# GpSimd makes a row's product in four pieces, one piece between two gathers that it issues

## The chip, the cores and the metric

The kernel runs on one core of one Trainium2 chip. The metric is the device time of one execution in microseconds (us), lower is better. The kernel before takes 3039.48 us, the median of three runs (3039.14 to 3041.27).

## The reference, cut to what matters

Two transformer blocks on 256 tokens of width 2048. The last step of the second block is a lookup among 16,384 experts, each with one row in the table `u` and one in the table `v` (2048 float32 values, 8 KB a row). For each token 8 heads pick 16 experts each, so 128 per token. A token's result is the sum over its experts of a weight times the `v` row, and the weight is the softmax gate times gelu of the dot product of the token's vector with the `u` row:

```python
def block(args):
    xb, eb, gb = args                     # 128 tokens
    a = jnp.einsum('nd,nhkd->nhk', xb, jnp.take(u_tab, eb, axis=0))
    w = (gb * jax.nn.gelu(a)).astype(xb.dtype)
    return jnp.einsum('nhk,nhkd->nd', w, jnp.take(v_tab, eb, axis=0))
```

The picks come from two rounds of top-16 per head over products of queries and keys.

## The kernel before, in words

The first 1750 us are dense products, whose weights stream in 1 MB chunks. The change lies in the lookup behind them.

**Tiles.** The 256 tokens are two blocks of 128, and a token is a partition. One "row" `q` of the kernel is a tile of 128 partitions by 2048 float32 (1 MB): slot `s` of all 128 tokens of a block, gathered by one indirect DMA that GpSimd issues (line 621). There are 512 rows in this order: 128 of `u` for block 0 (`q` 0 to 127), 128 of `v` for block 0, then the same for block 1.

**Buffers.** There are 14 row buffers (`GATH`). Row `q` goes into the buffer of row `q - 14`, so GpSimd waits before the gather of `q` until row `q - 14` is used (`row_free`). The gathers are issued in order, by one engine.

**Who uses a row.** A `u` row is multiplied with the token's vector and summed over its 2048 columns. VectorE does that in one instruction (`dot`, line 2677). Of the first 118 rows, those with `q % 6 == 3` (3, 9, ..., 117: 20 rows) are made by two other engines: GpSimd multiplies in place (line 606, `multiply`), and ScalarE adds up the product (line 1750), which sets the row free (`row_summed`). A `v` row is scaled and added by VectorE (line 2726), every fourth by TensorE through a diagonal matrix (line 1190).

**Order on GpSimd.** After the gather of row `q`, GpSimd makes the product of row `q - 8` if that is one of its rows. Before it, it waits until that row has landed. What stands behind it, the gather of `q + 1` first, waits until the product is done.

**What else VectorE does here.** Between its dot products it makes the picks of the heads in groups (`choose`), one step after every fourth slot: for the rest of block 0 while the `u` rows of block 0 come in, for block 1 while the `v` rows of block 0 do. The steps are the top-16 searches (lines 2612 to 2618), a cast of the positions (2628), candidate sums (2631), and the pick of the indices by comparison (2641 to 2653). The first three rows are dotted against the vector in SBUF, the others against a copy of it in PSUM (`xn_ps`).

Of the kernel before, what the change touches and what calls it, by code (L numbers as in the profile page):

```python
# [7 lines left out]
ALU = mybir.AluOpType  # L8
# [13 lines left out]
CW = 512  # L22
# [49 lines left out]
ROW_CHUNK = (0, 0, 1, 1, 2, 2, 3, 3, 4, 4, 4, 4, 4, 4)  # L72
FIRST_ROWS = 3
SHARE = 4
POOL_SHARE, POOL_UNTIL, POOL_BEHIND = 6, 118, 8
GELU_AT, GATES_AT = 96, 60
LAST_ROWS = 12
GROUPS = 4
# [27 lines left out]
def used_by(plan, m):  # L106

    return max(p for p, (k, _) in enumerate(plan) if k == m) + 1
# [13 lines left out]
def ada_slot(c):  # L122

    return (c + 1) % ADA_SLOTS
# [79 lines left out]
def by_pool(q):  # L204

    return q < POOL_UNTIL and q % POOL_SHARE == POOL_SHARE // 2
# [11 lines left out]
def lin(const, i=None, step=0):  # L218

    return const if i is None else i * step + const  # L220


def build(nc, a, out):
    with ExitStack() as ctx:
        sems = {}

        def sem(name):
            if name not in sems:
                sems[name] = ctx.enter_context(nc.semaphore(name))
            return sems[name]  # L230
# [28 lines left out]
        def view(name, where, off, shape, dt=F32):  # L259
            return nc.alloc_sbuf_tensor_at(name, [P] + shape, dt, offset=arena_at + 4 * (region[where] + off))  # L260
# [113 lines left out]
        XN2 = view("XN2", "P", 0, [NB, D])  # L374
# [43 lines left out]
        def row(q):  # L418
            return rows_g[:, ROW_AT[q % GATH], :]

        def row_landed(q):

            return sem(f"row_landed{q % GATH}"), 16 * (q // GATH + 1)

        def row_free(q):

            if by_tensor(q):
                return split_used, NCH + consumed(q)
            if by_pool(q):
                return sem("row_summed"), consumed(q)  # L430
            return sem("row_used"), consumed(q)
# [109 lines left out]
        @block.gpsimd  # L541
        def _(pool):
            pool.wait_ge(x_landed[X_PARTS - 1], 16)
            pool.dma_start(wa[:, :, :], a["wa"]).then_inc(sem("mixer_landed"), 16)
            pool.dma_start(wx[:, :, :], a["wx"]).then_inc(sem("mixer_landed"), 16)
            pool.dma_start(decay[:, :, :], a["decay"]).then_inc(sem("mixer_landed"), 16)
            pool.dma_start(rope[:, :, :, :], a["rope"]).then_inc(sem("mixer_landed"), 16)

            pool.wait_ge(sem("ret_s_ready"), 4)
            for dst, name in ((pool_t, "pool_t"), (sgu_w, "sgu_w"), (pool_w, "pool_w"), (keys, "keys"), (mask, "mask"),  # L550
                              (wg, "wg")):
                pool.dma_start(dst[tuple(slice(None) for _ in dst.shape)], a[name]).then_inc(sem("tables_landed"), 16)
            pool.wait_ge(sem("y1_ready"), 2 * LB)
            pool.dma_start(c_row[:, :, :].rearrange("p r k -> p (r k)"), a["c_rows"].partition_broadcast(P)).then_inc(
                sem("c_row_landed"), 16)

            def load_ada(c, s):
                pool.dma_start(ada_w[s][:, :], a["ada"][c]).then_inc(ada_landed[s], 16)  # L558

            for c in range(ADA_SLOTS):  # L560
                load_ada(c, ada_slot(c))
            pool.dma_start(fnw[:, :], a["fnw"].partition_broadcast(P)).then_inc(sem("tables_landed"), 16)
            for c in range(ADA_SLOTS, C_STEP):
                before = c - ADA_SLOTS
                if before < C_FIRST:
                    pool.wait_ge(sem("ada_dots"), used_by(ADA_OUT, before))
                else:
                    pool.wait_ge(sem("ada_dots"), D_FIRST + used_by(ADA_FIRST, before - C_FIRST))
                load_ada(c, ada_slot(c))
            with pool.Fori(0, ADA_LOOPS) as i:  # L570
                for m in range(9):
                    if m < ADA_SLOTS:
                        used = used_by(ADA_STEP, 9 + m - ADA_SLOTS)
                    else:
                        used = D_STEP + used_by(ADA_STEP, m - ADA_SLOTS)
                    pool.wait_ge(sem("ada_dots"), lin(used, i, len(ADA_STEP)))
                    load_ada(lin(C_STEP + m, i, 9), ada_slot(C_STEP + m))
            for m in range(len(ADA_END)):
                if m < ADA_SLOTS:
                    used = D_END - len(ADA_STEP) + used_by(ADA_STEP, 9 + m - ADA_SLOTS)  # L580
                else:
                    used = D_END + m - ADA_SLOTS + 1
                pool.wait_ge(sem("ada_dots"), used)
                load_ada(C_END + m, ada_slot(C_END + m))

            pool.wait_ge(sem("ada_dots"), ADA_DOTS)
            pool.dma_start(ctx_x[:, :, :], a["ctx"].rearrange("o (b p) d -> p (o b) d", p=P)).then_inc(
                sem("ctx_landed"), 16)
            pool.wait_ge(sem("mod_kept"), 1)
            for r in range(4):  # L590
                pool.dma_start(mod_rows[r, :].rearrange("(k p) -> k p", p=P), mod_t[0:KT, r, :]).then_inc(sem("rows_stored"), 16)
            pool.wait_ge(sem("cols_ps"), 2)
            pool.dma_start(sgu_n[:, :], a["sgu_n"].partition_broadcast(P)).then_inc(sem("ctx_landed"), 16)
            pool.wait_ge(sem("rows_stored"), 16 * 4)
            pool.wait_ge(sem("h_ready"), NB * 2 * MH)
            for r, made in enumerate((gb1, gb2)):
                pool.dma_start(made[:, :], mod_rows[r, :].partition_broadcast(P)).then_inc(sem("rows_loaded"), 16)
            pool.wait_ge(sem("rows_loaded"), 16 * 2)
            pool.wait_ge(sem("y2_ready"), KT)
            for r, made in enumerate((sc_row, sh_row)):  # L600
                pool.dma_start(made[:, :], mod_rows[2 + r, :].partition_broadcast(P)).then_inc(sem("rows_loaded"), 16)

            def multiply(q):
                pool.wait_ge(*row_landed(q))
                pool.wait_ge(sem("xn2_ready"), 1)
                pool.tensor_tensor(row(q), row(q), XN2[:, 0, :], ALU.mult).then_inc(sem("pool_made"), 1)  # L606

            for p, (table, b) in enumerate((("u_tab", 0), ("v_tab", 0), ("u_tab", 1), ("v_tab", 1))):
                for s in range(SLOTS):
                    q = p * SLOTS + s  # L610
                    if table == "u_tab" and s % GSTEP == 0:
                        pool.wait_ge(sem("idx_ready"), b * GROUPS + s // GSTEP + 1)
                        pool.sem_inc(sem("gathers"), 1)
                    if q < GATH:
                        if not ROW_CHUNK[q]:
                            pool.wait_ge(sem("xn2_ready"), NB)
                        pool.wait_ge(split_used, NCH - SLOTS_W + ROW_CHUNK[q])
                    else:
                        pool.wait_ge(*row_free(q - GATH))
                    pool.sem_inc(sem("gathers"), 1)  # L620
                    pool.indirect_dma_start(  # L621
                        out=row(q), out_offset=None, in_=a[table],
                        in_offset=bass.IndirectOffsetOnAxis(ap=idx[:, b, s:s + 1], axis=0),
                    ).then_inc(row_landed(q)[0], 16)
                    if q >= POOL_BEHIND and by_pool(q - POOL_BEHIND):
                        multiply(q - POOL_BEHIND)
            pool.wait_ge(sem("sum_kept"), 1)
            pool.tensor_tensor(gated_v[:, 1, :], gated_v[:, 1, :], gb2[:, :], ALU.mult).then_inc(sem("pool_made"), 1)
            pool.wait_ge(sem("pool_made"), POOL_MADE + 1)
            pool.tensor_tensor(X[:, NB - 1, :], X[:, NB - 1, :], gated_v[:, 1, :], ALU.add).then_inc(sem("pool_made"), 1)  # L630
# [1176 lines left out]
        def _(dve):  # L1807
# [492 lines left out]
            def updates(S, steps, banks=ALLB):  # L2300

                u0, depth = upd[0], len(banks) // MKT
                todo = [(d, n, h) for _, d, n in steps for h in range(MH)]

                def weigh(q):
# [583 lines left out]
```

## Time and profile before

| | us |
|---|---|
| median of the runs | 3039.48 |
| profiled execution | 3039.09 |
| its span, first to last instruction | 3037.3 |
| GpSimd busy in the span | 654.1 |
| VectorE busy in the span | 2463.1 |
| product on GpSimd, 128 x 2048, 20 of them, mean | 4.524 |
| issue of a gather of `u` on GpSimd, 256 of them, mean | 0.976 |
| dot product on VectorE, 128 x 2048, mean | 2.285 |
| sum on ScalarE, 128 x 2048, 20 of them, median | 1.912 |

The page gives a busy share for each engine and for 40 equal slices of the span. GpSimd's issue of a gather counts as busy there; the transfer itself is in the lines DMA and GB/s. The whole-span shares average stages with different limits, so the views that count are those of the stretch in which the 20 products are made, 1740 us to 2040 us.

### The profile page before, as it was taken

Reading aid. Unit: us, or ns where it says so; the run is one execution under the profiler, and the core shown is the slowest. Engines: PE = TensorE matmul, PEld = TensorE weight load, DVE = VectorE, ACT = ScalarE, POOL = GpSimd, SP = SyncE. Lnnn points to the kernel's source line nnn. Section 1 sums busy time; section 2 is a strip of 40 time slices with the busy share of each in tenths; the row PEclk is TensorE's granted clock in tenths of the full one; section 3 lists DMA queues with packets and bytes.
Section 4 is the critical chain, followed back from the end, with each engine's and each line's share of the span. In section 5 each row is a group of like instructions: output and inputs, shape, how many; then the busy total and the mean of one; then the engine's idle time right before and its main releaser. Section 6 shows DMA issues by size and latency. Waiting matters only on the chain.

```text
span 3037.3 us, 24749 instructions
## 1 busy us (share of the span) xinstructions
PE 2115.9 (70%) x8578; PEld 1586.2 (52%) x8578; DVE 2463.1 (81%) x2630; ACT 888.1 (29%) x931; POOL 654.1 (22%) x656
## 2 busy tenths in 40 slices
PE   9999999999999999999999910004656200015653
PEld 7888888888888887888788800001212000002221
DVE  6675688999999887575566899979997899987677
ACT  5544443333334366534455311110000000000001
POOL 0000000000000000000000176773333343333332
PEclk9999999999999999999999955556676655557676
DMA  6454778888988965344354699999999999999997
GB/s 247 173 199 168 296 270 321 330 339 333 337 329 328 343 242 174 145 153 156 125 208 166 223 415 396 418 422 421 421 422 422 422 422 422 422 422 422 421 421 307
DMA packets 133192, 958.53 MB, mean 316 GB/s; under 512 B 14833, under 2 KB 15153, under 8 KB 17137
## 3 DMA queue, kind: packets, MB, share of 16 engines
q0 software_dynamic: 89824, 650.98, 52.7%
q1 hardware_dynamic: 43136, 305.91, 27.4%
q8 instruction: 49, 0.80, 0.1%
q10 hardware_dynamic: 146, 0.53, 0.0%
q14 instruction: 37, 0.30, 0.0%
HBM read 955.23 MB, written 2.13 MB: 315 GB/s over the span
## 4 chain that ended last, share of the span: by engine, by line
PE 57%; DMA 25%; DVE 13%; issue 3%; POOL 2%; ACT 1%; SPq 0%; POOLq 0%; DVEq 0%; ACTq 0%
DMA rows_g<-in_v_tab_dram,idx 18%; PE bank L647 17%; PE bank L651 17%; PE bank L648 17%; DVE rows_g L2677 8%; DMA rows_g<-in_u_tab_dram,idx 6%; PE bank L1190 2%; POOL rows_g L621 2%; PE bank L681 1%; DVE bank L2726 1%; PE bank L1004 0%; DMA raw<-in_wstream_dram 0%; PE bank L950 0%; PE bank L689 0%; PE bank L860 0%
## 5 line engine op out<-in xcount | busy, mean ns | idle before, releaser
L1815 DVE TENSOR_TENSOR WL<-raw,WH 128x2048 fp32r<-128x2048 f32 x287 | 657.1, 2291 | 290.7 <-ACT WH L1204 284.8
L1190 PE MATMUL bank<-rows_g,diag 128*128 128x512 f32 x488 | 363.9, 915 | 725.2 <-DMA rows_g<-in_v_tab_dram,idx 725.2
L647 PE MATMUL bank<-WH,UH 128*128 128x512 f32 x1952 | 770.4, 395 | 3.3 <-DVE WL L1815 2.9
L651 PE MATMUL bank<-WH,UL 128*128 128x512 f32 x1952 | 761.1, 390 | 0.0
L648 PE MATMUL bank<-WL,UH 128*128 128x512 f32 x1952 | 760.3, 389 | 0.0
L1204 ACT ACTIVATE WH<-raw 128x2048 fp32r<-128x2048 f32 x287 | 550.3, 1918 | 679.3 <-DMA raw<-in_wstream_dram 665.8
L1190 PEld LDWEIGHTS bank<-rows_g,diag 128*128 128x128 f32 x488 | 139.2, 299 | 950.7 <-issue 660.3
L2677 DVE CUSTOM_DVE_ANT_0 rows_g<-rows_g,bank 128x2048 f32<-128x2048 f32 x233 | 524.8, 2285 | 36.6 <-DMA rows_g<-in_u_tab_dram,idx 36.0
L2726 DVE SCALAR_TENSOR_TENSOR bank<-rows_g,gate_w,bank 128x2048 f32<-128x2048 f32 x193 | 454.5, 2355 | 116.5 <-DMA rows_g<-in_v_tab_dram,idx 98.1
L647 PEld LDWEIGHTS bank<-WH,UH 128*128 128x128 f32 x1952 | 367.0, 188 | 79.6 <-issue 2.6
L651 PEld LDWEIGHTS bank<-WH,UL 128*128 128x128 f32 x1952 | 366.7, 188 | 76.9
L648 PEld LDWEIGHTS bank<-WL,UH 128*128 128x128 f32 x1952 | 367.1, 188 | 74.6
L621 POOL DMA_INDIRECT rows_g<-in_u_tab_dram,idx x256 | 249.8, 976 | 432.7 <-DVE dots L2677 201.7
L621 POOL DMA_INDIRECT rows_g<-in_v_tab_dram,idx x256 | 241.7, 944 | 389.0 <-PE bank L1190 217.2
L2090 DVE CUSTOM_DVE_ANT_0 ada_out<-ada_w,c_row 128x2048 f32<-128x2048 f32 x128 | 292.6, 2286 | 0.0
L558 POOL DMA_DIRECT2D ada_w<-in_ada_dram x96 | 50.9, 530 | 697.7 <-DVE ada_sum L2090 697.7
L1767 ACT ACTIVATE diag<-ident,gate_w 128x128 f32<-128x128 f32 x61 | 24.4, 402 | 555.1 <-PE bank L1190 554.6
L647 PE MATMUL bank<-WH,FH 128*128 128x512 f32 x320 | 124.7, 390 | 1.5 <-DVE X L2158 1.5
L651 PE MATMUL bank<-WH,FL 128*128 128x512 f32 x320 | 124.5, 389 | 0.0
L648 PE MATMUL bank<-WL,FH 128*128 128x512 f32 x320 | 124.5, 389 | 0.0
L1750 ACT ACTIVATE rows_g<-rows_g 128x2048 f32<-128x2048 f32 x20 | 38.2, 1911 | 235.4 <-POOL rows_g L606 235.4
L1178 PE MATMUL bank<-nfin,ident 1*128 1x512 f32 x8 | 7.2, 1076 | 142.5 <-DMA nfin<-in_nfin_dram 142.5
(409 smaller groups left out, 1618.2 us busy)
## 6 DMA issues: line engine op xcount, KB each, us to landing
raw<-in_wstream_dram SPq DMA_DIRECT2D x288, 1024.0 KB, 4.9
ada_w<-in_ada_dram POOLq DMA_DIRECT2D x96, 1024.0 KB, 7.5
rows_g<-in_u_tab_dram,idx POOLq DMA_INDIRECT x256, 24.0
rows_g<-in_v_tab_dram,idx POOLq DMA_INDIRECT x256, 30.1
X<-in_x_dram SPq DMA_DIRECT2D x4, 512.0 KB, 9.9
c_row<-in_c_rows_dram POOLq DMA_DIRECT2D x1, 2048.0 KB, 8.6
ctx_x<-in_ctx_dram POOLq DMA_DIRECT2D x1, 2048.0 KB, 10.4
gb<-mod_rows POOLq DMA_DIRECT2D x2, 1024.0 KB, 5.6
```

The source lines that it names most:

```text
L558: pool.dma_start(ada_w[s][:, :], a["ada"][c]).then_inc(ada_landed[s], 16)
L621: pool.indirect_dma_start(out=row(q), out_offset=None, in_=a[table], in_offset=bass.IndirectOffsetOnAxis(ap=idx[:, b, s:s + 1], axis=0),). ...
L647: pe.matmul(o, ah[:, k0 + k, t], wh[:, w], start=first and k == 0, stop=False)
L648: mm = pe.matmul(o, ah[:, k0 + k, t], wl[:, w], start=False, stop=al is None and last and k == nk - 1)
L651: mm = pe.matmul(o, al[:, k0 + k, t], wh[:, w], start=False, stop=last and k == nk - 1)
L1190: mm = pe.matmul(bank[c], diag[:, n % 2, :], row(q)[:, c * CW:(c + 1) * CW], start=s == mine[0], stop=s == mine[-1])
L1204: act.activation(WH[:, n % SLOTS_W, :], raw[:, n % SLOTS_W, :], ACT.Copy).then_inc(hi_ready, 1)
L1750: act.activation(row(q), row(q), ACT.Copy, accum_out=dots[:, 0, q:q + 1]).then_inc(sem("row_summed"), 1)
L1815: dve.tensor_tensor(WL[:, n % SLOTS_W, :], raw[:, n % SLOTS_W, :], WH[:, n % SLOTS_W, :].bitcast(F32), ALU.subtract).then_inc(lo_ready, 1)
L2090: dve.tensor_tensor_reduce(ada_out[:, :], ada_w[ada_slot(c)][:, :], c_row[:, r, :], 1.0, 0.0, ALU.mult, ALU.add, ada_sum[:, p:p + 1]).then ...
L2677: dve.tensor_tensor_reduce(row(q), row(q), x, 1.0, 0.0, ALU.mult, ALU.add, dots[:, b, q % SLOTS:q % SLOTS + 1]).then_inc(sem("row_used"), 1)
L2726: ins = dve.scalar_tensor_tensor(v_ps, row(q), w, v_ps, ALU.mult, ALU.add)
```

## The change

GpSimd's product of a row is cut into four instructions of 512 columns (`CW`). The first comes after the gather of `q + 7` (it was `q + 8` for the whole), the second after `q + 8`, the third after `q + 9`, the fourth after `q + 10`. Only the first waits for the row to land, and only the fourth counts up `pool_made`, for which ScalarE's sum waits. The arithmetic is the same, and so is everything on the other engines.

```diff
-POOL_SHARE, POOL_UNTIL, POOL_BEHIND = 6, 118, 8
+POOL_SHARE, POOL_UNTIL, POOL_BEHIND, POOL_PIECES = 6, 118, 7, 4
@@
-            def multiply(q):
-                pool.wait_ge(*row_landed(q))
-                pool.wait_ge(sem("xn2_ready"), 1)
-                pool.tensor_tensor(row(q), row(q), XN2[:, 0, :], ALU.mult).then_inc(sem("pool_made"), 1)
+            def multiply(q, piece):
+                w = slice(piece * CW, (piece + 1) * CW)
+                if piece == 0:
+                    pool.wait_ge(*row_landed(q))
+                    pool.wait_ge(sem("xn2_ready"), 1)
+                ins = pool.tensor_tensor(row(q)[:, w], row(q)[:, w], XN2[:, 0, w], ALU.mult)
+                if piece == POOL_PIECES - 1:
+                    ins.then_inc(sem("pool_made"), 1)
@@
-                    if q >= POOL_BEHIND and by_pool(q - POOL_BEHIND):
-                        multiply(q - POOL_BEHIND)
+                    for piece in range(POOL_PIECES):
+                        made = q - POOL_BEHIND - piece
+                        if made >= 0 and by_pool(made):
+                            multiply(made, piece)
```

## Rows read from the trace of the kernel before

**Rows 1.** The page, span by slices: DMA share in tenths, GB/s, then VectorE and GpSimd.
```profile
DVE  6675688999999887575566899979997899987677
...
POOL 0000000000000000000000176773333343333332
...
DMA  6454778888988965344354699999999999999997
GB/s 247 173 199 168 296 270 321 330 339 333 337 329 328 343 242 174 145 153 156 125 208 166 223 415 396 418 422 421 421 422 422 422 422 422 422 422 422 421 421 307
```

**Rows 2.** Windows of the lookup: busy us (count) of each engine, granted clock, DMA share, GB/s.
```profile
1745.00:1747.50 2.50, 2.50 (x13) 2.07 (x12) 2.50 (x3) 0.00 (x0) 2.19 (x2) 1.00 0.53 128
...
1750.00:1760.00 10.00, 5.72 (x24) 5.06 (x24) 7.80 (x11) 4.26 (x6) 8.79 (x6) 0.57 1.01 393
1760.00:1850.00 90.00, 0.00 (x0) 0.00 (x0) 89.14 (x148) 12.30 (x13) 61.22 (x42) 0.50 1.01 422
1850.00:1910.00 60.00, 7.19 (x8) 2.49 (x8) 59.41 (x73) 9.04 (x10) 40.10 (x28) 0.50 0.98 384
1910.00:2040.00 130.00, 0.00 (x0) 0.00 (x0) 110.28 (x101) 23.21 (x23) 94.00 (x66) 0.50 1.01 422
2040.00:2980.00 940.00, 351.08 (x472) 134.26 (x472) 805.24 (x721) 31.51 (x72) 362.28 (x380) 0.64 1.01 422
```

**Rows 3.** Chain that ended last, its last pieces: start us, us, what.
```profile
2991.21 30.02 DMA rows_g<-in_v_tab_dram,idx
...
3021.25 2.37 DVE bank L2726
```

**Rows 4.** Timeline of VectorE: start us, us, line, operation, tiles, shapes.
```profile
1754.38 4.52 DVE L2649 SCALAR_TENSOR_TENSOR pick_f<-exp_f,exp_f 128x32 f32<-128x32 f32 x1 [2.03 <-ACT bank L1724]
...
1762.36 2.29 DVE L2677 CUSTOM_DVE_ANT_0 rows_g<-rows_g,bank 128x2048 f32<-128x2048 f32 x1
1764.58 0.08 DVE L2677 DVE_READ_ACCUMULATOR2_ANT dots<- 128x1 f32 x1
1764.58 2.28 DVE L2677 CUSTOM_DVE_ANT_0 rows_g<-rows_g,bank 128x2048 f32<-128x2048 f32 x1
...
1779.91 3.25 DVE L2628 CAST top_f<-top_i 128x64 f32<-128x64 uint32 x1
...
1812.69 3.24 DVE L2641 TENSOR_SCALAR pick_i<-best_i 128x32 uint32<-128x32 uint32 x1
...
1828.65 2.29 DVE L2677 CUSTOM_DVE_ANT_0 rows_g<-rows_g,bank 128x2048 f32<-128x2048 f32 x1
...
1878.99 3.24 DVE L2641 TENSOR_SCALAR pick_i<-best_i 128x32 uint32<-128x32 uint32 x1
```

**Rows 5.** Timeline of GpSimd, same columns.
```profile
1754.30 4.54 POOL L606 TENSOR_TENSOR rows_g<-rows_g,XN 128x2048 f32<-128x2048 f32 x1
1759.00 0.97 POOL L621 DMA_INDIRECT rows_g<-in_u_tab_dram,idx  x1 [0.16 <-issue]
1760.28 0.95 POOL L621 DMA_INDIRECT rows_g<-in_u_tab_dram,idx  x1 [0.30 <-issue]
...
1766.21 4.54 POOL L606 TENSOR_TENSOR rows_g<-rows_g,XN 128x2048 f32<-128x2048 f32 x1
...
1778.59 4.51 POOL L606 TENSOR_TENSOR rows_g<-rows_g,XN 128x2048 f32<-128x2048 f32 x1
...
1811.37 4.51 POOL L606 TENSOR_TENSOR rows_g<-rows_g,XN 128x2048 f32<-128x2048 f32 x1
...
1959.10 4.51 POOL L606 TENSOR_TENSOR rows_g<-rows_g,XN 128x2048 f32<-128x2048 f32 x1 [3.02 <-DMA rows_g<-in_u_tab_dram,idx]
...
1973.99 4.51 POOL L606 TENSOR_TENSOR rows_g<-rows_g,XN 128x2048 f32<-128x2048 f32 x1 [3.03 <-DMA rows_g<-in_u_tab_dram,idx]
```

**Rows 6.** One line of the kernel: operation and count, ns min/median/max, first and last start.
```profile
L2628 DVE CAST top_f<-top_i x8: 186/188/3254, 1700.2 to 2269.2; 128x64 f32<-128x64 uint32 x8
L2641 DVE TENSOR_SCALAR pick_i<-best_i x16: 173/176/3242, 1709.6 to 2298.8; 128x32 uint32<-128x32 uint32 x16
L2649 DVE SCALAR_TENSOR_TENSOR pick_f<-exp_f,exp_f x8: 184/186/4523, 1724.6 to 2308.7; 128x32 f32<-128x32 f32 x8
```

**Rows 7.** GpSimd's groups by line and shape: busy us, mean ns, idle before.
```profile
L606 POOL TENSOR_TENSOR rows_g<-rows_g,XN 128x2048 f32<-128x2048 f32 x20 | 90.5, 4524 | 20.8 <-DMA rows_g<-in_u_tab_dram,idx 20.5
...
L591 POOL DMA_DIRECT2D mod_rows<-mod_t x4 | 2.0, 496 | 55.4 <-ACT mod_t L1541 55.4
```

## The prediction

> **What bounds the kernel now.** I read three views in this order. The slices of the page come first [rows 1]: from the 24th slice on (1746 us) the DMA engines are full and move 421 or 422 GB/s, except in the 24th (415), the 25th (396), the 26th (418) and the last. So the lookup is paced by its transfers. One row is 1.0486 MB, so at 422 GB/s it takes 2.485 us, and 512 rows take 1272 us. The windows then show where the pace is lost [rows 2]. From 1760 to 1850 it is 422. From 1850 to 1910 it is 384. From 1910 to 2040 and from there to 2980 it is 422 again. The chain at the end confirms it [rows 3]: the last 30.02 us before VectorE's last product are a transfer of a `v` row. A microsecond of lost transfer in the lookup is therefore a microsecond of the kernel, and an engine that is faster where the pace is already 422 gives nothing.
>
> The third view is the reason for the loss. In 1850 to 1910 VectorE is busy 59.41 of 60 us, in 1760 to 1850 89.14 of 90 [rows 2]. It has more to do per row than a transfer takes, so it falls behind until the 14 buffers hold landed rows that it hasn't used, and GpSimd can't issue the next gather. One group of picks takes the 24 slots from the dot that starts at 1762.36 to the one at 1828.65 [rows 4]: 66.29 us, against 24 x 2.485 = 59.64 us of transfers. VectorE loses 6.65 us to them there, and the same again in the next group. A dot costs 2.21 us (the step from its row to the next in [rows 4], 20 dots are 44.2 us), and 22.1 us are picks.
>
> Part of these 22.1 us isn't work. Three small instructions, of 32 or 64 columns, take 0.18 to 0.19 us in the median and 3.24 to 4.52 at the most [rows 6]. The long ones all coincide with a product on GpSimd. The cast starts at 1779.91 and ends at 1783.16; the product runs from 1778.59 to 1783.10. The scalar operation runs 1812.69 to 1815.93, the product 1811.37 to 1815.88. The one at 1754.38 starts 0.08 us after the product at 1754.30 and lasts as long [rows 4, 5]. So a VectorE instruction of that kind waits until GpSimd's product is over. There are five: one of 4.34 us over its own time, and four (about 1780, 1813, 1846, 1879) of 3.06 each, 16.6 us in all. The dots, whose second operand is in PSUM, keep 2.28 us beside a product.
>
> **The change part by part.**
>
> 1. *The length of a hold on VectorE.* A piece is a quarter of the product. Its price isn't in the trace, so I bound it. The floor is 4.524 / 4 = 1.13 us [rows 7]. For the ceiling I take a fixed part as long as this engine's shortest whole DMA issue in those groups, 0.496 us: 0.496 + (4.524 - 0.496) / 4 = 1.50 us. I take 1.2, near the floor, since a product starts within 0.02 us of the issue before it [rows 5] and shows no gap of its own. The five waits become at most 1.2 each. I expect other instructions of the picks to meet pieces, since pieces are spread over four gathers: pieces run 4.8 of every 14.9 us, so a third of the four clusters of exposed instructions per group meets one, for 0.6 us in the mean, or twice that if two pieces hit one cluster: 1 to 2 us per group where 6.12 stood. VectorE's 66.29 us become 66.29 - 6.12 + 1.5 = 61.7, and it falls behind by 2.0 us a group, 4 in both.
>
> 2. *What is late next.* The buffers took up the whole lag from 1762 to 1850, about 6.65 + 1 us, before a gather came late. A lag of 4 us, from a start that is 4.34 - 1.2 = 3.1 us earlier, never reaches that. So the loss in 1850 to 1910 goes, all of it: 60 x (422 - 384) / 422 = 5.4 us. That is the main term, and its cap. The 12.2 us that VectorE saves on the four waits are not the gain; past the point where transfers are full again, VectorE just waits for rows.
>
> 3. *The length of a hold on the gathers.* Before, the next gather was 4.7 us behind (1754.30 to 1759.00 in [rows 5]), now at most a piece and 0.16 us. While transfers are full this is hidden by the 8 rows in flight. In 1850 to 1910 it adds to the same loss, and can't be counted again. In 1750 to 1760 the pace is 393 [rows 2], a loss of 10 x 29 / 422 = 0.7 us around the first product, after which three gathers stand. I take a third of it, 0.2, with 0 and 0.7 as ends, because TensorE's last products (5.72 us busy) fall there too. The 128 GB/s at 1745 [rows 2] are before the first piece and stay.
>
> 4. *GpSimd's own load.* Product and six issues, back to back, take 1766.21 - 1754.30 = 11.91 us [rows 5], so the six issues take 7.37. With four pieces of 1.2 the cycle is 12.2, with 1.5 it is 13.4. The transfers allow 6 x 2.485 = 14.91, which is the step from 1959.10 to 1973.99 [rows 5]. Below that it costs nothing; the cover is gone at a piece of 1.89 us.
>
> 5. *The wait that moves.* The wait for landing now stands after gather `q + 7`. Where transfers pace, GpSimd waits there (3.02 us at 1959.10 [rows 5]), and the gathers behind it wait with it. At that moment 7 rows are in flight instead of 8, 17.4 us of transfers, and the next gather follows after 1.4 us. Nothing runs dry: 0 us.
>
> 6. *The row that comes free later.* The last piece ends after gather `q + 10`, about 8.5 us behind the first one's start instead of 4.5, then 1.9 us of sum (the table above). The gather of `q + 14` is three issues behind, 3.7 us, and needs 1.9. 0 us, at most 0.3 where a wait for VectorE doesn't cover it.
>
> 7. *After 2040* no product is cut, VectorE has idle time, and the pace is 422 [rows 2]. What is won stays won.
>
> The Trainium skill (SBUF — State Buffer, "Who interferes with whom") says that VectorE and GpSimd share a pair of ports, that a VectorE instruction with two SBUF inputs or in a two-port mode competes for it, and that whoever starts first has it for the whole instruction. The trace agrees: the waits above last to the end of a product. By that rule a piece caps a wait at its own length, as in step 1.
>
> The skill also has a rule against the change: GPSIMD Engine Reference, "3.1 Elementwise — side-by-side cycle accounting", lists two software hops per instruction and a join of eight cores as costs beyond the 2.6 cycles an element. As an estimate from its figures, 4497 ns less 2048 x 2.6 / 1.2 GHz leaves 0.06 us of fixed cost, so a piece of 1.17 us; 60 more instructions would be 3.6 us on GpSimd, all of it under the cover of step 4. The trace has one size only and can't show it.
>
> **Sum.** 3039.09 - 5.4 - 0.2 = 3033.5 us for the profiled execution (1.8 us around its span included). The median of the runs lies 0.39 above that execution, so 3033.9.
>
> **The rivals.**
>
> - *Half the loss stays.* If pieces meet the picks more often (3 to 4 us per group), VectorE's lag reaches some 8 us at the end of the second group, and about half of the loss returns. For it: the waits before were in step with the products, four of the same length, so chance isn't the right measure. Against: even so each is short. 3039.5 - 2.8 = 3036.7.
> - *No gain.* The picks alone take 16.0 us of VectorE per group, 44.2 + 16.0 = 60.2 against 59.64, and if the starting lag fills the buffers by itself, the loss stays where it is: 3039.3. Against: the pace holds 422 for 90 us under a lag growing by 1 us in 10.
> - *Slower, by collisions.* The place is VectorE's picks between 1760 and 1900. There are four clusters of instructions per group that read through what GpSimd holds. If every one of them meets two pieces, of 1.35 us (the middle of my bounds), that is 8 x 1.35 = 10.8 us a group, 21.6 in two and 1.35 at the start, against 16.6 now: 6.35 us more on an engine that already holds back the gathers. 3045.8. It decides from about 4.5 full hits a group on (6.12 / 1.35). For it: two pieces can fall in one cluster, since a piece comes every 2.4 us and a cluster lasts 2 to 3. Against: two of four clusters a group were free of any wait although products covered 30% of the time.
> - *The pieces don't do what they say* would be a cost of over 1.89 us each, with GpSimd as the bound. I count it into the slower case.
>
> **Chances.** Forecast 0.70, half loss 0.14, no gain 0.08, slower 0.08. A difference of 0.2% (6.1 us) is about what a measurement of this kernel can tell from no change. The forecast's gain, 5.4 to 6.1 by its terms and some 0.7 either way by scatter, lies right at that mark: I give 0.36 of its 0.70 to faster by over 0.2% and 0.34 to less. With the next two cases and a quarter of the last, within 0.2% has 0.58; slower by over 0.2% has 0.06. The forecast's own range is 3032.6 to 3035.3. The range that leaves out the slower case and the outer part of the others is 3032.2 to 3039.0.
>
> **What would show each step right or wrong.** The longest of lines 2628, 2641 and 2649 should fall from 3.2 and 4.5 us to 1.4 or less. A piece should read 1.13 to 1.5 us. The window from 1850 to 1910 should show about 422 GB/s with VectorE waiting for landed rows in it. The 24 slots of a group should take near 60 us, paced by transfers. If the window still shows 384 with short waits, step 2 is wrong; if the pieces read 1.9 us or more, step 4. If the time falls by more than 6.5 us, transfers were lost somewhere that I counted as full.

## The result

The kernel is 0.16% faster. In 12 runs of each, the changed kernel takes 3035.26 us in the median and the kernel before 3040.85. The ratio on record is 0.9984 with a 95% interval of 0.9977 to 0.9992, so 2 to 7 us less, some 4.9 (the two medians by themselves are 5.6 apart). The forecast was 5.6 us less, at 3033.9. The difference is clear of zero, but smaller than 0.2% (6.1 us).

The profiled execution of the changed kernel takes 3032.99 us, with a span of 3031.3, 6.0 us less than before. Not all of that is the change's. The dense part is the same code, and in this profile its end came earlier: the first gather starts at 1724.15 us instead of 1726.25. In the 14 profiles of this study that start lies anywhere from 1722.9 to 1731.1. So that part is scatter, and I compare the **lookup** alone, from the start of the first gather to the landing of the last row. It repeats to 0.6 us in two profiles of the kernel before (run 1). Before it is 3021.22 - 1726.25 = 1294.97 us [rows 3], after it 3015.21 - 1724.15 = 1291.06, which is 3.9 us less.

The page of the changed kernel, VectorE, GpSimd and transfers by slices, as in [rows 1]:

```profile
DVE  6675689999999987675566899889997899987677
...
POOL 0000000000000000000000077773333343333332
...
DMA  6454778888888964444354699999999999999997
GB/s 248 174 199 167 296 268 324 328 334 341 333 336 326 350 239 172 148 153 156 125 208 167 222 411 421 421 422 422 421 421 422 422 422 422 422 422 421 422 422 297
```

The 25th slice, 396 GB/s before, now has 421. The windows show the same beside [rows 2]:

```profile
1760.00:1850.00 90.00, 0.00 (x0) 0.00 (x0) 89.10 (x148) 13.59 (x14) 68.19 (x62) 0.50 1.01 422
1850.00:1910.00 60.00, 7.19 (x8) 2.49 (x8) 59.52 (x64) 9.60 (x10) 47.53 (x44) 0.50 1.01 422
1910.00:2040.00 130.00, 0.00 (x0) 0.00 (x0) 108.34 (x99) 21.35 (x21) 96.08 (x89) 0.50 1.01 422
2040.00:2980.00 940.00, 345.50 (x479) 132.40 (x480) 801.97 (x716) 31.24 (x70) 359.43 (x378) 0.66 1.01 422
```

The 60 us at 384 GB/s are gone. VectorE is still busy in 59.52 of them, but it no longer holds back the transfers. Its timeline, the rows that answer to [rows 4] (line numbers are six higher here):

```profile
1752.74 1.99 DVE L2659 CAST idx<-pick_f 128x32 uint32<-128x32 f32 x1
1757.76 2.29 DVE L2683 CUSTOM_DVE_ANT_0 rows_g<-rows_g,bank 128x2048 f32<-128x2048 f32 x1
...
1806.24 1.18 DVE L2647 TENSOR_SCALAR pick_i<-best_i 128x32 uint32<-128x32 uint32 x1
1808.39 1.95 DVE L2651 TENSOR_TENSOR hot<-hot,top_f 128x512 f32<-128x512 f32 x1
...
1821.39 2.29 DVE L2683 CUSTOM_DVE_ANT_0 rows_g<-rows_g,bank 128x2048 f32<-128x2048 f32 x1
```

And GpSimd where the three long instructions stand, as in [rows 5]:

```profile
1752.41 0.97 POOL L625 DMA_INDIRECT rows_g<-in_u_tab_dram,idx  x1 [0.16 <-issue]
1753.40 1.28 POOL L608 TENSOR_TENSOR rows_g<-rows_g,XN 128x512 f32<-128x512 f32 x1
...
1806.09 1.28 POOL L608 TENSOR_TENSOR rows_g<-rows_g,XN 128x512 f32<-128x512 f32 x1
1807.53 0.97 POOL L625 DMA_INDIRECT rows_g<-in_u_tab_dram,idx  x1 [0.16 <-issue]
1808.52 1.27 POOL L608 TENSOR_TENSOR rows_g<-rows_g,XN 128x512 f32<-128x512 f32 x1
```

A piece takes 1.28 us. The scalar operation that starts at 1806.24 ends at 1807.42, 0.05 us behind the piece that it met. The one at 1808.39 meets the next piece and waits 1.26 us over its 0.69. So the cluster meets two pieces, and waits 2.3 us in all where it waited 3.06. A group of picks now takes 1821.39 - 1757.76 = 63.63 us, against 66.29 before.

A wait isn't always as short as a piece. The cast at 1752.74 starts under the issue of a gather, 0.66 us ahead of the piece at 1753.40, and still ends behind that piece, at 1754.73: 1.99 us for a cast that takes 0.18 elsewhere.

### The profile page after: what moved, and what is told of

Its sections match the earlier page's. It is cut to its first block, busy times and chain, and to the rows that moved or that the text cites. A ratio compares the mean times of both kernels' runs of the same rounds, so it can differ in the third digit from the quotient of the medians.

```text
span 3031.3 us, 24809 instructions
## 1 busy us (share of the span) xinstructions
PE 2103.0 (69%) x8578; PEld 1581.3 (52%) x8578; DVE 2456.7 (81%) x2630; ACT 886.7 (29%) x931; POOL 666.6 (22%) x716
## 4 chain that ended last, share of the span: by engine, by line
PE 58%; DMA 24%; DVE 12%; issue 3%; POOL 3%; ACT 1%; SPq 0%; POOLq 0%; DVEq 0%; ACTq 0%
DMA rows_g<-in_v_tab_dram,idx 19%; PE bank L653 17%; PE bank L657 17%; PE bank L654 17%; DVE rows_g L2683 8%; DMA rows_g<-in_u_tab_dram,idx 5%; PE bank L1196 2%; POOL rows_g L625 2%; POOL rows_g L608 1%; PE bank L687 1%; DVE bank L2732 1%; PE bank L1010 0%; PE bank L956 0%; PE bank L695 0%; PE bank L866 0%
## 5 line engine op out<-in xcount | busy, mean ns | idle before, releaser
L1196 PE MATMUL bank<-rows_g,diag 128*128 128x512 f32 x488 | 351.9, 888 | 735.5 <-DMA rows_g<-in_v_tab_dram,idx 735.5
L608 POOL TENSOR_TENSOR rows_g<-rows_g,XN 128x512 f32<-128x512 f32 x80 | 102.2, 1277 | 21.8 <-DMA rows_g<-in_u_tab_dram,idx 20.4
L1756 ACT ACTIVATE rows_g<-rows_g 128x2048 f32<-128x2048 f32 x20 | 38.2, 1910 | 234.5 <-POOL rows_g L608 234.5
```

Of the source, the lines that this page charges most:

```text
L608: ins = pool.tensor_tensor(row(q)[:, w], row(q)[:, w], XN2[:, 0, w], ALU.mult)
L1196: mm = pe.matmul(bank[c], diag[:, n % 2, :], row(q)[:, c * CW:(c + 1) * CW], start=s == mine[0], stop=s == mine[-1])
```

## The experiments

I state the theory in terms of VectorE. Over the two groups of picks (48 rows from the dot behind one group's indices to the dot behind the next but one's) the transfers need 48 x 2.485 = 119.3 us. The more VectorE's **two groups** take over that, the more it lags; some of the lag is taken up by the buffers, the rest is a loss. The rivals are that GpSimd's hold on the gathers makes the loss, that the position alone does it, and that the transfers' mean loss isn't what the end sees.

Runs 2, 3 and 4 were executed ten times each, the others once, with the profile. Their whole times mean little, since the dense part scatters by some 8 us: the kernel of run 6 took 3035.73 us and the kernel before beside it 3040.41, although its lookup is the slower one. Those runs are read by the lookup of one profile, and differences of about 0.6 us in it say nothing.

All in us. "Window" is the GB/s from 1850 to 1910; the lookup is measured to the last landing, in the runs behind `q + 6` and with 32 pieces to the start of VectorE's last product, which is within 0.03 us of it elsewhere.

| kernel | two groups | window | lookup |
|---|---|---|---|
| before | 66.29 + 63.17 = 129.46 | 384 | 1294.97 |
| before, once more | 129.41 | 387 | 1294.39 |
| changed (4 pieces, from q+7) | 63.63 + 60.34 = 123.97 | 422 | 1291.06 |
| position only (whole, q+7) | 64.57 + 60.68 = 125.25 | 422 | 1291.53 |
| cut only (4 in a row, q+8) | 67.08 + 63.96 = 131.04 | 370 | 1298.38 |
| no product | 60.14 + 57.25 = 117.39 | 422 | 1291.21 |
| hold on the gathers only | 60.15 + 57.03 = 117.18 | 421 | 1290.94 |
| work in place of the waits | 66.71 + 63.59 = 130.30 | 386 | 1294.93 |
| whole, q+6 | 62.96 + 57.21 = 120.17 | 422 | 1292.87 |
| 2 pieces, from q+7 | 65.68 + 59.77 = 125.45 | 422 | 1290.72 |
| 8 pieces, from q+5 | 63.73 + 58.61 = 122.34 | 422 | 1291.09 |
| 32 pieces, 8 in a row | 62.09 + 60.30 = 122.39 | 388 | 1314.69 |

**1. The kernel before, once more.** No edit.

> The kernel before, once more, to see how far its lookup repeats. I measure the lookup from the start of the first gather to the landing of the last row: 1726.25 to 3021.22 = 1294.97 us before, 1724.15 to 3015.21 = 1291.06 us after the change, 3.91 us less, where the prediction had 5.6. Either theory: if the lookup repeats to within 0.5 us (and the same window of some 60 us shows about 384 GB/s), the 3.9 us are the change's and the 2.09 us by which the first gather came earlier are chance of the dense part. If it moves by 2 us or more, one profile of each can't carry the comparison.

The lookup is 1294.39, 0.6 us off the first profile, and the window shows 387. So 3.9 us are the change's to within some 0.6, and the 2.1 us of the earlier start are not.

**2. Position only.** The product whole, one gather earlier.

```diff
-POOL_SHARE, POOL_UNTIL, POOL_BEHIND = 6, 118, 8
+POOL_SHARE, POOL_UNTIL, POOL_BEHIND = 6, 118, 7
```

> The product whole, but behind gather q+7 instead of q+8: the position alone. Theory (the length of the holds is what mattered): the lookup stays within 1 us of 1295.0, the long small VectorE instructions still last up to 3 or 4.5 us, only in other places. Rival (the position shifted the products out of step with the picks, and that alone removed the waits): no instruction of lines 2628 and 2641 over 1 us, 422 GB/s throughout, lookup near 1291.

I expected no change from it. It gives nearly all that the change gives: lookup 1291.53, and in ten runs 3037.25 us, a ratio to before of 0.9988 (0.9978 to 0.9998). The rival was right on the time and only half right on the way. The waits don't go; they get shorter. VectorE's timeline, then GpSimd's, of this kernel:

```profile
1814.47 2.00 DVE L2641 TENSOR_SCALAR pick_i<-best_i 128x32 uint32<-128x32 uint32 x1
```

```profile
1811.90 4.52 POOL L606 TENSOR_TENSOR rows_g<-rows_g,XN 128x2048 f32<-128x2048 f32 x1
1816.58 0.97 POOL L621 DMA_INDIRECT rows_g<-in_u_tab_dram,idx  x1 [0.16 <-issue]
```

Before, the product began 1.32 us ahead of this operation (1811.37 and 1812.69 in [rows 4, 5]), now 2.57 us. The two engines run in step, because GpSimd's gathers wait for VectorE's dots, so one issue earlier (1.24 us) is 1.24 us less to wait: 3.24 became 2.00 at three of the four places. At the fourth, the cast at 1782.15, only half a microsecond is gained (2.78 us), and the first wait of all falls from 4.52 to 3.27.

What the cut adds to the position isn't shown. The lookups of this kernel and the changed one are 0.5 us apart, and the ratios 0.9988 and 0.9984 have intervals that overlap.

**3. Cut only.** Four pieces behind `q + 8`, with no gather between them.

```diff
-                    for piece in range(POOL_PIECES):
-                        made = q - POOL_BEHIND - piece
-                        if made >= 0 and by_pool(made):
+                    made = q - POOL_BEHIND      # POOL_BEHIND is 8
+                    if made >= 0 and by_pool(made):
+                        for piece in range(POOL_PIECES):
                             multiply(made, piece)
```

> Four pieces, but all four behind gather q+8, with nothing between them: GpSimd holds the gathers for 4 x 1.28 = 5.1 us as a block, while VectorE can slip in between two pieces. Theory A (the waits of VectorE's small instructions were the cause): each wait at most 1.3 us, lookup within 1 us of 1291.1. Theory B (the hold on the gathers was the cause): 1295 or somewhat more, since the hold is 0.6 us longer than before, with the dips of the window still there. If VectorE can't slip in between pieces, its waits stay near 3 us and the run says nothing between the two.

It is slower than before: 3043.06 us in ten runs, ratio 1.0011 (1.0001 to 1.0020), lookup 1298.38. VectorE doesn't get in between two pieces. GpSimd's timeline, then VectorE's:

```profile
1813.27 4.92 POOL L608 TENSOR_TENSOR rows_g<-rows_g,XN 128x512 f32<-128x512 f32 x4
1818.35 0.97 POOL L625 DMA_INDIRECT rows_g<-in_u_tab_dram,idx  x1 [0.16 <-issue]
```

```profile
1814.59 3.65 DVE L2647 TENSOR_SCALAR pick_i<-best_i 128x32 uint32<-128x32 uint32 x1
```

The small operation waits to the end of all four, 0.4 us longer than for the whole product. So this run can't part theory A from B, as its expectation had said for that case. What it shows is that the cut by itself is worth nothing: four pieces back to back hold VectorE like one product.

**4. No product.** GpSimd waits for the row and counts up, without multiplying. The 20 rows are summed unmultiplied.

```diff
-                pool.tensor_tensor(row(q), row(q), XN2[:, 0, :], ALU.mult).then_inc(sem("pool_made"), 1)
+                pool.sem_inc(sem("pool_made"), 1)
```

> The kernel before with GpSimd's products left out (the 20 rows are summed without being multiplied), everything else and all waits in place: no hold on VectorE and none on the gathers. It is the ceiling of what any cutting can bring. Theory (the change already has all of it, what remains of the 5.6 predicted is not there to be had): lookup 1290.5 to 1291.5, window at 422 GB/s. Rival (the pieces still cost something): 1289.5 or less.

The lookup is 1291.21, and ten runs give 3036.92 us, a ratio of 0.9984 (0.9975 to 0.9994), the same as the change's. That is the ceiling, and the changed kernel has reached it (1291.06), to within what the lookup repeats. The groups take 60.14 and 57.25, so without any wait the first group is as long as the prediction had worked out (60.2), the second 2.9 us shorter. In the changed kernel 3.5 and 3.1 us of waits a group are left, and they cost nothing.

**5. Hold on the gathers only.** To part the two holds, GpSimd waits where the product was, but touches no memory.

```diff
 # on top of the kernel without products
                 pool.sem_inc(sem("pool_made"), 1)
+                if q >= 4:
+                    pool.wait_ge(*row_free(q - 4))
```

> The product left out as in the run without products (lookup 1291.21), but GpSimd is held at the same 20 places: it waits there until VectorE has used row q-4, two dots past the one that released the gather before, 4.4 us while VectorE is behind. So the gathers are held about as long as by a product, and nothing of VectorE's is held. Theory A (the lag of VectorE, made of its own waits, costs the time): group of picks in 60.1 us, 422 GB/s in the 60 us window, lookup 1291.2 within 0.5. Theory B (the hold on the gathers costs it): dips in the window, lookup 1293 or more.

The lookup is 1290.94 us. But the hold is shorter than the expectation has it. GpSimd's timeline at one of the 20 places, in the kernel without products and then in this one:

```profile
1792.49 0.94 POOL L621 DMA_INDIRECT rows_g<-in_u_tab_dram,idx  x1 [0.30 <-issue]
1795.17 0.94 POOL L621 DMA_INDIRECT rows_g<-in_u_tab_dram,idx  x1 [1.75 <-DVE dots L2677]
```

```profile
1791.80 0.94 POOL L623 DMA_INDIRECT rows_g<-in_u_tab_dram,idx  x1 [0.30 <-issue]
1796.71 0.94 POOL L623 DMA_INDIRECT rows_g<-in_u_tab_dram,idx  x1 [3.98 <-DVE dots L2679]
```

The step from one gather to the next is 4.91 us here and 2.68 without the hold. At eight of the 20 places the step is 3.2 to 6.9 us, 0.9 to 2.2 more than without the hold, and at the others there is no difference; a whole product makes such a step 5.65 us. So 2 us more of hold cost nothing while VectorE doesn't lag. For the hold of a whole product this run doesn't show it. Run 2 does: the product there is whole, the step is 5.65 us as before, and the window is at 422 all the same.

**6. Work in place of the waits.** The reverse: GpSimd holds nothing, and VectorE works where it had waited. `stand_in(n)` is two sums over `n` columns of PSUM into a spare cell.

```diff
 # on top of the kernel without products
+                if b == 0 and g >= 2:
+                    stand_in(1392)
                 link.mark(dve.tensor_copy(top_f[:, :, :], top_i[:, :, :]))
@@
+                    if b == 0 and g >= 2 and s == 1:
+                        stand_in(1392)
                     link(dve.tensor_scalar(pick_i[:, :], ranks, by, None, op))
@@
+                if b == 0 and g == 1:
+                    stand_in(2048)
                 link(dve.scalar_tensor_tensor(pick_f[:, :], exp_f[0]...
```

> The product left out again, but VectorE gets added work where it had waited: two reductions of 1392 columns (some 3.1 us) before the same four instructions of the last two groups of picks, and two of 2048 (some 4.4 us) before the fifth in the group ahead. GpSimd never holds anything. Theory A (only VectorE's lost time counts): groups of 66.3 and 63.2 us as before, a window near 384 GB/s, lookup back at 1294.4 to 1295.0. Theory B (the holds on the gathers are needed for the loss): lookup 1291.2 to 1292.5.

The whole loss is back: 1294.93 us. Windows of run 5, then of this run:

```profile
1850.00:1910.00 60.00, 7.19 (x8) 2.49 (x8) 59.52 (x66) 9.60 (x10) 24.52 (x26) 0.50 1.01 421
```

```profile
1850.00:1910.00 60.00, 7.19 (x8) 2.47 (x8) 59.41 (x67) 9.61 (x10) 23.51 (x25) 0.50 0.97 386
```

VectorE is as busy in the one as in the other, so its busy time doesn't tell them apart; the GB/s do. Runs 2, 4 and 6 settle the cause. VectorE's lost time makes the loss, without any hold by GpSimd (run 6); GpSimd's hold on the gathers doesn't make it alone (run 2). How much the two add to each other when VectorE does lag stays open: the cut in a row lags only 0.7 us more than run 6 and loses 3.5 us more.

**7 and 8. One drain, early and late.** The lookup gained 3.9 us, not the 5.6 of the lost GB/s. To see what the end counts, I emptied the transfers once, in the changed kernel.

```diff
 # behind the gather of row q; late: q == 470
+                    if q == 130:
+                        pool.wait_ge(*row_landed(q))
```

> The changed kernel (lookup 1291.06) with one more wait: after the gather of q = 130 GpSimd waits until that very row has landed, which empties all transfers once, and then issues on. Theory S (one of the 16 DMA engines carries some 9 us more over the lookup, by the 0.25 MB of instruction packets, lies behind the others and sets the end; the mean GB/s counts idle time of the other 15 that costs nothing): the end moves by the refill alone, 2 to 4 us, the mean loses 1 to 2 us more than that, and the tail after the last full slice gets a little shorter. Rival M (a microsecond of lost mean transfer is a microsecond at the end): end and mean loss move by the same.

> The same wait after the gather of q = 470. Theory S: the lagging engine is then some 8 us behind, so the mean loses about 7 us more than the early one's refill, but the end moves by the same 2 to 4 us as with the early one, and the tail (from the last slice at 400 GB/s or more to the last landing, 8.2 us before and 10 after the change) shrinks to 1 to 3 us. Rival M: the tail stays 8 to 10 us and the end moves by as much as the mean loses.

The lookups are 1294.15 (+3.1) and 1297.16 (+6.1). The loss in the mean GB/s, summed over slices of 10 us against 422 and without the last 35 us, is 5.4 us more than in the changed kernel in the early one and 11.7 in the late one. The late drain, in windows:

```profile
2902.00:2906.00 4.00, 1.93 (x4) 0.53 (x2) 3.74 (x3) 0.40 (x1) 0.00 (x0) 0.90 0.86 358
2906.00:2910.00 4.00, 2.35 (x3) 1.18 (x4) 1.54 (x1) 0.00 (x0) 0.00 (x0) 0.52 0.14 59
2910.00:2914.00 4.00, 3.99 (x6) 1.25 (x4) 3.80 (x2) 0.00 (x0) 0.00 (x0) 0.62 0.06 27
2914.00:2918.00 4.00, 0.00 (x0) 0.00 (x0) 3.26 (x2) 0.40 (x1) 1.87 (x2) 0.80 0.21 35
```

A DMA share of 0.06 is one engine of 16. From about 2906 on, 14 engines had nothing more to do while one or two were still moving rows for some 8 us. In the early drain the same takes 2 us at a share near 0.1. The tails say it again. The changed kernel at its end, then the kernel with the late drain:

```profile
3003.00:3005.00 2.00, 0.00 (x0) 0.00 (x0) 2.00 (x1) 0.00 (x0) 0.00 (x0) 0.50 0.97 401
3005.00:3007.00 2.00, 0.00 (x0) 0.00 (x0) 1.87 (x2) 0.00 (x0) 0.00 (x0) 0.50 0.42 176
3007.00:3009.00 2.00, 0.00 (x0) 0.00 (x0) 1.90 (x2) 0.00 (x0) 0.00 (x0) 0.50 0.15 61
...
3013.00:3015.00 2.00, 0.00 (x0) 0.00 (x0) 2.00 (x1) 0.00 (x0) 0.00 (x0) 0.50 0.05 20
```

```profile
3017.00:3019.00 2.00, 0.00 (x0) 0.00 (x0) 1.87 (x2) 0.00 (x0) 0.00 (x0) 0.50 1.04 434
3019.00:3021.00 2.00, 0.00 (x0) 0.00 (x0) 1.86 (x2) 0.00 (x0) 0.00 (x0) 0.50 0.50 205
3021.00:3023.00 2.00, 0.00 (x0) 0.00 (x0) 2.00 (x1) 0.00 (x0) 0.00 (x0) 0.50 0.05 20
```

The tail is 10 us without a drain and 3 us behind the late one. Rival M, that mean and end move together, falls in both runs. Theory S holds for the lagging engine and its tail, but not for its number: the late drain costs the end 3 us more than the early one, where S had them equal. Those 3 us are open.

What makes an engine fall behind, the trace shows too. Each gather reports in 16 parts, one from each engine, and the packed trace keeps the times (no view prints them). In run 2, which has them all, the last part of row 131 comes 2.25 us behind the first part, and that of the last row 9.28 us. In between the lag grows in seven steps of 0.95 to 1.02 us (at rows 136, 164, 200, 239, 300, 354 and 437), each 1.5 to 2.7 us after the start of an instruction packet of 8192 bytes. Between them it stays level, but for a passing rise around row 294, so an engine that is steadily slower than the others isn't what makes it. The second last part has steps of its own, of about 0.65 us, behind other packets of the same kind, and ends at 5.48 us. The other profiles that have all the times show such steps too. The trace doesn't name the engine of a part, so that it is the same engine each time is inferred from the growth.

**9. Whole product behind q+6.**

```diff
-POOL_SHARE, POOL_UNTIL, POOL_BEHIND = 6, 118, 8
+POOL_SHARE, POOL_UNTIL, POOL_BEHIND = 6, 118, 6
```

> The product whole, behind gather q+6. The picks took 60.1 us a group without products, 66.3 and 63.2 with the product behind q+8, 64.6 and 60.7 behind q+7. Theory (what counts is by how much VectorE falls behind the transfers over the two groups, and some 6 us of it cost nothing): if the two groups sum to 126 us or less, the lookup is 1291 to 1292 and the window at 422 GB/s; at 129 or more it is 1294 or more. Rival (the position matters in itself, since an earlier product holds the gathers when fewer are in flight): 1293 or more even with groups summing to 126.

The two groups sum to 120.17, the shortest of all with a product, and yet the lookup is 1292.87: between the two expectations, next to the rival's. GpSimd now often comes to the product before the row has landed. Its waits from 1728 to 2040 us:

```profile
POOL rows_g L606 <- DMA rows_g<-in_u_tab_dram,idx: 41.8, 16, 4.0
```

Before there were 7 such waits and 20.5 us in all [rows 7], late in the stage, with the transfers full. But these waits aren't what costs. The first of them stands at 1792.86, with the fourth product, and the pace is lost before it:

```profile
1754.00:1764.00 10.00, 5.72 (x24) 5.05 (x24) 7.83 (x25) 5.91 (x7) 8.51 (x7) 0.66 0.90 339
1764.00:1774.00 10.00, 0.00 (x0) 0.00 (x0) 9.93 (x21) 2.06 (x3) 8.90 (x6) 0.55 0.98 395
1774.00:1784.00 10.00, 0.00 (x0) 0.00 (x0) 9.95 (x10) 1.43 (x1) 8.91 (x6) 0.50 1.01 425
```

The first whole product runs from 1754.18 to 1758.71 there, behind the tenth gather (row 9), and the next gather waits for it. That is what the rival names, a hold on the gathers while few are in flight. It fits that in the 10 us that begin 30 us after the first gather the rate is 324 GB/s here and 363 in run 2, but 407 without products and 425 in the changed kernel, whose pieces let the next gather go. No run moved the first product alone, so this is argued and not shown.

**10 and 11. Two pieces, eight pieces.**

```diff
-POOL_SHARE, POOL_UNTIL, POOL_BEHIND, POOL_PIECES = 6, 118, 7, 4
+POOL_SHARE, POOL_UNTIL, POOL_BEHIND, POOL_PIECES = 6, 118, 7, 2    # or 5, 8
@@
-                w = slice(piece * CW, (piece + 1) * CW)
+                w = slice(piece * D // POOL_PIECES, (piece + 1) * D // POOL_PIECES)
```

> Two pieces of 1024 columns, behind q+7 and q+8. From 4.524 us for 2048 columns and 1.277 for 512, a column costs 2.11 ns and an instruction 0.2 us, so a piece is 2.36 us. Theory (lag): groups between those of the whole product behind q+7 and those of four pieces, sum 124 to 126 us, lookup 1291 to 1291.6. Rival: longer holds bring dips back, 1292.5 or more.

> Eight pieces of 256 columns, one behind each of q+5 to q+12. A piece is 0.2 + 256 x 2.11 ns = 0.74 us, GpSimd's cycle 7.4 + 8 x 0.64 = 12.5 to 12.8 us of 14.9. Theory (lag, with many short waits): groups sum to 121 to 124 us, lookup 1291 within 0.5, no gain over four pieces, since four have all that is to be had. Rival: the row comes free only after gather q+12 and its sum of 1.9 us, the gather of q+14 waits for it and the lookup is 1293 or more.

1290.72 and 1291.09: both at the ceiling, within what the lookup repeats. The products by shape, two pieces and then eight:

```profile
L608 POOL TENSOR_TENSOR rows_g<-rows_g,XN 128x1024 f32<-128x1024 f32 x40 | 94.3, 2358 | 23.3 <-DMA rows_g<-in_u_tab_dram,idx 22.6
```

```profile
L608 POOL TENSOR_TENSOR rows_g<-rows_g,XN 128x256 f32<-128x256 f32 x160 | 116.1, 737 | 22.4 <-DMA rows_g<-in_u_tab_dram,idx 19.4 <-DVE dots L2683 1.0
```

2.36 and 0.74 us are what a fixed 0.2 us and 2.11 ns a column give. Two, four and eight pieces can't be told apart, and no number can beat them by much, since no product at all is no faster.

**12. 32 pieces, eight in a row behind each of q+7 to q+10.**

```diff
-POOL_SHARE, POOL_UNTIL, POOL_BEHIND, POOL_PIECES = 6, 118, 7, 4
+POOL_SHARE, POOL_UNTIL, POOL_BEHIND, POOL_PIECES = 6, 118, 7, 32
@@
-                w = slice(piece * CW, (piece + 1) * CW)
+                w = slice(piece * D // POOL_PIECES, (piece + 1) * D // POOL_PIECES)
@@
-                        made = q - POOL_BEHIND - piece
+                        made = q - POOL_BEHIND - piece // 8
```

> 32 pieces of 64 columns, eight behind each of q+7 to q+10, to find where GpSimd becomes the bound. Eight pieces in a row cost 8 x (0.135 + 0.13) = 2.1 us by the four in a row that took 4.92, at most 8 x 0.33 = 2.7 with the 0.2 us of a piece by itself. The cycle of six gathers is then 7.4 + 4 x 2.1 - 0.4 = 15.4 to 17.8 us, where transfers allow 14.91. Theory (step 4 of the prediction): the 20 products take 19 x (0.5 to 2.9) = 9 to 55 us longer, all of it at the end: lookup 1300 to 1346. Rival (something else covers it): 1295 or less.

1314.69 us, 23.6 more than with four pieces, within what step 4 had led me to expect. GpSimd's timeline shows the cycle:

```profile
1800.28 2.26 POOL L608 TENSOR_TENSOR rows_g<-rows_g,XN 128x64 f32<-128x64 f32 x8
...
1816.87 2.26 POOL L608 TENSOR_TENSOR rows_g<-rows_g,XN 128x64 f32<-128x64 f32 x8
```

Six gathers take 16.59 us there, where the transfers allow 14.91; 19 such cycles would be 32 us, so not all of it comes through. The pace falls to between 381 and 394 GB/s in all windows from 1750 to 2040, and VectorE is busy only 53 of 60 us in the window from 1850.

## Why the prediction was right or wrong

- **The number: in part luck.** The medians of the runs fell by the 5.6 us of the forecast, the ratio on record says 4.9, and the lookup, where the change lies, fell by 3.9. The rest can't be told from the scatter of the dense part.
- **What bounds the lookup: right.** Full transfers, but for 60 us in which VectorE lags. Runs 4 and 6 show it both ways: take VectorE's waits away and 422 GB/s are there, put the same time back as work and the loss is back.
- **Step 1, the price of a piece: right, the waits that stay: too low.** 1.28 us lies in the bounds of 1.13 to 1.50, a little above the 1.2 taken; the fixed cost is 0.2 us and not the 0.06 of the prediction's estimate. The waits left are 3.5 and 3.1 us a group, not 1.5: in both groups the same two clusters meet pieces, and one of them meets two. The rival "half the loss stays" named just this amount, and it didn't come, because the picks without waits are shorter in the second group (57.25) than I had taken them (60.2). So "the same again in the next group" was wrong as well: before the change the second group took 63.17 us and lost 3.5 us to the transfers, not 6.65.
- **Step 1, a wait at most as long as a piece: not quite.** The long instructions of the three lines named are now 1.35, 1.18 and 0.19 us, under the 1.4 forecast. But the cast of line 2659 at 1752.74 takes 1.99 us, since it begins under the gather's issue before the piece.
- **Step 1, the cause of the shorter wait: incomplete.** I put it all on the length of the piece. Run 2 shows that the move from `q + 8` to `q + 7`, which I had costed only as a wait for landing, gets 3.4 of the 3.9 us by itself (2.9 of 3.3 against the second profile of the kernel before); run 3 shows that the cut without a gather between pieces gets less than nothing.
- **Step 2, the lag under the slack: right.** I had VectorE 4 us behind over two groups; it is 123.97 - 119.3 = 4.7, and the pace holds 422. At 6.0 (position only) there is hardly a loss, at 10.2 one of 3.3 to 3.9. One sign didn't come: VectorE was to wait for landed rows between 1850 and 1910, and it is busy for 59.52 of the 60 us. A lag under the slack of the buffers is enough.
- **Step 2, its size: the term that was mis-sized.** The window did go from 384 to 422, all of it, but 60 x 38 / 422 = 5.4 us of mean transfers were 3.9 us at the end, with step 3's 0.2 in them. The premise that failed is the prediction's "a microsecond of lost transfer in the lookup is therefore a microsecond of the kernel". The mean is over 16 DMA engines. The end waits for the one that lies furthest behind, and that one is less idle while the rate is low: its lag (last part behind first, see behind runs 7 and 8) at row 131 is 1.5 us in run 1 and 1.9 in run 6, which have the 60 us of low rate, but 2.8 in run 4 and 3.1 in run 5, which don't. The tail shows it: from the last window near 400 GB/s to the last landing it took 8 us before and 10 us after, so most engines finished 5.9 us earlier in the lookup (by windows of 2 us) and the last row 3.9.
- **Steps 4, 6 and 7: right.** GpSimd has room in its cycle of a product and six gathers: 12.2 us in the changed kernel, as forecast, and 13.5 with eight pieces cost nothing, 16.59 do (run 12). Where between them the cost begins no run shows. The later release costs nothing (even with eight pieces), and 422 GB/s stand after 2040.
- **Step 5: right.** The wait for landing costs nothing at `q + 7`. At `q + 6` the lookup is 1.8 us longer than in the changed kernel, but the pace is lost before the first such wait. The likelier place is step 3, the first product's hold on the gathers (run 9).
- **The slower rival** didn't happen here, but its mechanism is real: run 3 is slower by waits on collisions.

## What to carry to other kernels

When two engines share something and also wait for each other, their collisions are in step: most have the same length every time, and moving an issue by one place changes nearly all of them at once, so try the order before the cut. Here the move of one issue gave what could be told from the noise, and the cut alone gave nothing. If you cut, don't issue the pieces back to back. And a drop in mean transfer rate is a ceiling for the gain, not the gain: look at the tail of the transfers to see how far one engine lies behind the others.

## What the runs showed of the hardware

VectorE's small operations wait to the end of four back-to-back products of GpSimd (3.65 us in the timeline of run 3), and got in behind one piece where a gather followed it (1.18 us in the changed kernel). The Trainium skill (SBUF — State Buffer, "Who interferes with whom") says that the first of the two has the ports "for the whole instruction". The trace agrees for single products; that four in a row act as one, it doesn't say. Nor does the first to start always win: the operation at 1808.39 starts 0.13 us before the piece at 1808.52, and it is the one that waits (1.26 us), while the piece takes its usual 1.27.

A product on GpSimd costs 4.52, 2.36, 1.28 and 0.74 us for 2048, 1024, 512 and 256 columns: 2.11 ns a column and 0.2 us fixed, but in a row only 4.92 - 4.52 = 0.4 us for three more.

Over the lookup the last DMA engine falls some 8 to 10 us behind the first, and the second last 4 to 6, in steps that follow the packets of instructions (run 2, behind runs 7 and 8). In the kernel before, from 1750 to 2990 us, these are:

```profile
q14 instruction: 19, 0.16, 0.0%
q8 instruction: 4, 0.07, 0.0%
```

All 0.23 MB at one engine's 422 / 16 = 26.4 GB/s would be 8.7 us, but that isn't how the lag comes about. A packet of 8192 bytes would be 0.31 us by that rate, and a step is about 1 us on the one engine and 0.65 on the other. That the packets make the steps is inferred from their times; no run here took them away.
